# First expert's rows gathered by halves, scattered rows read back by the sync engine, one weight split moved: a two-layer diffusion block on one Trainium2 core

## The reference, cut to what matters

```python
def grouped_moe(h, router_w, router_b, w_gate, w_up, w_down):
    ...
    _, idx = lax.top_k(jnp.where(in_group, biased, NEG_INF), TOP_K)   # two experts of each token
    w = jnp.take_along_axis(scores, idx, axis=-1)
    w = w / jnp.sum(w, axis=-1, keepdims=True)
    ...
    hid = jax.nn.silu(jnp.einsum('td,edf->tef', ht, w_gate)) * jnp.einsum('td,edf->tef', ht, w_up)
    y = jnp.einsum('tef,efd->td', hid * gates[:, :, None], w_down)
```

## Time and profile before

| | |
|---|---|
| median of 3 runs | 849.35 us (847.86 to 852.73) |
| profiled execution | 854.77 us, its span 852.9 us |
| PE busy | 766.4 us (90%) |
| DVE / ACT / POOL busy | 522.3 / 470.0 / 192.3 us |
| mean granted PE clock | 0.933 |

### The profile page before, as it was taken

How to read it: one execution, slowest core, us unless ns; L and a number is a source line. 1 busy time by engine, 2 the same in 40 slices (tenths; PEclk the granted TensorE clock), 3 DMA queues, 4 the chain that set the end, 5 groups by cost and what they waited for, 6 DMA issues and landing times.

```text
span 852.9 us, 13041 instructions
## 1 busy us (share of the span) xinstructions
PE 766.4 (90%) x4850; PEld 608.9 (71%) x4850; DVE 522.3 (61%) x769; ACT 470.0 (55%) x664; POOL 192.3 (23%) x181
## 2 busy tenths in 40 slices
PE   4599999999999748999999739999999799999995
PEld 3278867856787637888888526898569588888883
DVE  2254333349733635888889436753684758988884
ACT  3353221259613625888888427641773557767763
POOL 0103000630004035699942141303102000000000
PEclk9889999999999657999999959999999689999998
DMA  9992787895111155999999879941434038999942
GB/s 361 348 262 88 268 323 270 320 310 182 51 66 50 49 199 181 322 369 361 354 364 335 307 265 304 312 149 50 170 104 159 29 142 312 366 350 345 344 164 76
DMA packets 88385, 200.06 MB, mean 235 GB/s; under 512 B 19410, under 2 KB 45564, under 8 KB 88316
## 3 DMA queue, kind: packets, MB, share of 16 engines
q1 hardware_dynamic: 81696, 185.17, 61.2%
q0 software_dynamic: 4608, 8.40, 2.8%
q10 hardware_dynamic: 2012, 5.61, 1.7%
HBM read 196.00 MB, written 11.53 MB: 243 GB/s over the span
## 4 chain that ended last, share of the span: by engine, by line
PE 66%; POOL 8%; DVE 8%; ACT 6%; DMA 6%; issue 4%; SPq 0%; ACTq 0%; POOLq 0%; DVEq 0%
PE bank L1368 13%; PE bank L1369 12%; PE bank L1370 12%; POOL onehot L875 4%; PE bank L1396 4%; DMA y_rows<-y_sb,idx_row 3%; PE bank L1525 2%; POOL x_row L885 2%; PE bank L1526 2%; PE bank L1527 2%; PE bank L1672 2%; PE bank L1698 2%; PE bank L1684 2%; DVE w_lo L2342 2%; POOL y_rows L891 1%
## 5 line engine op out<-in xcount | busy, mean ns | idle before, releaser
L2342 DVE TENSOR_TENSOR w_lo<-raw,w_hi 128x2048 fp32r<-128x2048 f32 x96 | 219.8, 2293 | 16.6 <-ACT w_hi L1234 15.8
L1234 ACT ACTIVATE w_hi<-raw 128x2048 fp32r<-128x2048 f32 x96 | 184.1, 1919 | 37.8 <-PE bank L1370 37.8
L1368 PE MATMUL bank<-h_hi,w_hi 128*128 128x512 f32 (+2 forms) x288 | 104.0, 361 | 6.4 <-DVE h_lo L2102 4.3
L1369 PE MATMUL bank<-h_lo,w_hi 128*128 128x512 f32 (+2 forms) x288 | 101.4, 352 | 0.0
L1370 PE MATMUL bank<-h_hi,w_lo 128*128 128x512 f32 (+2 forms) x288 | 101.3, 352 | 0.0
L1368 PE MATMUL bank<-w_hi,xg_hi 128*128 128x512 f32 x192 | 79.2, 413 | 2.6 <-DVE xg_lo L2506 2.6
L1369 PE MATMUL bank<-w_lo,xg_hi 128*128 128x512 f32 x192 | 76.6, 399 | 0.0
L1370 PE MATMUL bank<-w_hi,xg_lo 128*128 128x512 f32 x192 | 76.4, 398 | 0.0
L970 ACT ACTIVATE w_hi<-raw 128x2048 fp32r<-128x2048 f32 (+1 forms) x20 | 37.3, 1867 | 68.7 <-PE bank L1370 55.2
L2045 DVE TENSOR_TENSOR w_lo<-raw,w_hi 128x2048 fp32r<-128x2048 f32 (+1 forms) x20 | 44.9, 2247 | 48.4 <-ACT w_hi L970 48.2
L1368 PEld LDWEIGHTS bank<-h_hi,w_hi 128*128 128x128 f32 (+1 forms) x288 | 54.2, 188 | 16.5 <-issue 6.3
(11 more groups left out here) (326 smaller groups left out, 1547.5 us busy)
## 6 DMA issues: line engine op xcount, KB each, us to landing
raw<-in_ada_w SPq DMA_DIRECT2D x46, 1024.0 KB, 9.7
raw<-in_moe_w_gate SPq DMA_DIRECT2D x64, 512.0 KB, 5.1
raw<-in_moe_w_up SPq DMA_DIRECT2D x64, 512.0 KB
raw<-in_moe_w_down SPq DMA_DIRECT2D x64, 512.0 KB
raw<-in_w_in SPq DMA_DIRECT2D x14, 1024.0 KB, 10.9
raw<-in_w_out SPq DMA_DIRECT2D x8, 1024.0 KB, 9.3
ada_first<-in_ada_w SPq DMA_DIRECT2D x2, 1024.0 KB, 18.6
h_rows<-h_full SPq DMA_DIRECT2D x2, 1024.0 KB, 4.6
```

The lines of the kernel that those rows point to most:

```text
L1234: act.activation(w_hi[slot][:, :, :], raw[q][:, :, :], ACT.Copy).then_inc(split_hi, 1)
L1368: pe.matmul(dst, w_hi_, x_hi_, start=first, stop=False)
L1369: pe.matmul(dst, w_hi_, x_lo_, start=False, stop=False)
L2342: dve.tensor_tensor(w_lo[slot][:, :, :], raw[q][:, :, :], w_hi[slot][:, :, :].bitcast(F32), ALU.subtract).then_inc(split_lo, 1)
```

## The change

It has three parts and some renamed semaphores.

1. SP stores each column half twice: to its own tensor `h_half[half]` (T x 512), signalled by `h_first` or `h_second`, and to `h_rows` as before. POOL gathers experts 0 and 1 in four transfers of 2 KB rows: half 0 of both, then half 1 of both. PE, ACT and DVE turn and split half 0 of expert 0 first; PE multiplies role 0; then it turns half 1 of expert 0, then expert 1, and multiplies role 1. ACT's load of the SiLU table moves between the halves. Experts 2 to 15 are as before.
2. SP issues the read-back of `y_rows`, behind its six block loads. The lower half waits for all scatters but expert 15's, the upper for that one too. POOL runs `swap(1)` without a wait for the scatters. The sums are made by half tiles, 128x512: DVE makes the first, POOL the other seven.
3. DVE runs rows and modulation 1 ahead of `split(0, N_ADA)`, which moves behind the second `nx`.

```diff
@@ SP
                             sp.wait_ge(q_ta, l * KC + 4 * (half + 1))
+                            sp.dma_start(h_half[half].rearrange("(t p) d -> p t d", p=P), h_full[:, :, cs]).then_inc((h_first, h_second)[half], 16)
                             sp.dma_start(h_rows.rearrange("(t p) d -> p t d", p=P)[:, :, cs], h_full[:, :, cs]).then_inc(h_out, 16)
...
                         load_block(l + 1, q)
+                    rows = y_rows.rearrange("(i t p) d -> p t i d", i=2, p=P)
+                    sp.wait_ge(q_out[0], 16 * (E // 2) * k)
+                    sp.wait_ge(q_out[1], 16 * (E // 2) * k - 16)
+                    sp.dma_start(y_back[:, :, 0, :], rows[:, :, 0, :]).then_inc(q_lower, 16)
+                    sp.wait_ge(q_out[1], 16 * (E // 2) * k)
+                    for t in range(4):
+                        sp.dma_start(y_back[:, t, 1, :], rows[:, t, 1, :]).then_inc(q_back[t], 16)
@@ POOL
-                    gather(k, 0)
-                    gather(k, 1)
+                        gather(k, 0)
+                        gather(k, 1)
+                    else:
+                        for half in range(2):
+                            gather(0, 0, half)
+                            gather(0, 1, half)
...
-                def all_stored(n):
-                    pool.wait_ge(q_out[0], 16 * (E // 2) * n)
-                    pool.wait_ge(q_out[1], 16 * (E // 2) * n - 16)
-                    pool.sem_inc(y_in, 1)
-                    pool.wait_ge(q_out[1], 16 * (E // 2) * n)
-                    pool.sem_inc(y_in, 1)
+                def sum_rows():
                     swap(l + 1)
                     pool.wait_ge(q_lower, 16 * (l + 1))
-                    for t in range(nt):
-                        pool.wait_ge(q_back[t], 16 * (l + 1))
-                        pool.tensor_tensor(y_back[:, t, 0, :], y_back[:, t, 0, :], y_back[:, t, 1, :], ALU.add).then_inc(q_c, 1)
+                    for t, half in combine_units(l):
+                        if half == 0:
+                            pool.wait_ge(q_back[t], 16 * (l + 1))
+                        if (t, half) != (0, 0):
+                            hs = slice(half * 512, (half + 1) * 512)
+                            pool.tensor_tensor(y_back[:, t, 0, hs], y_back[:, t, 0, hs], y_back[:, t, 1, hs], ALU.add).then_inc(q_c, 1)
@@ ACT
-                    act.wait_ge(y_in, 2 * l - 1)
-                    act.dma_start(y_back[:, :, 0, :], rows[:, :, 0, :]).then_inc(q_lower, 16)
-                    act.wait_ge(y_in, 2 * l)
-                    for t in range(4):
-                        act.dma_start(y_back[:, t, 1, :], rows[:, t, 1, :]).then_inc(q_back[t], 16)
...
-                    tokens_in(0, 0)
+                        tokens_in(0, 0)
+                    else:
+                        tokens_in(0, 0, 0)
+                        act.activation(col[:, 45:46], eps, ACT.Silu)
+                        tokens_in(0, 0, 1)
@@ PE
                                 if role == 1 and e == 0:
+                                    if k == 0:
+                                        tokens(0, 0, 1)
                                     pe.wait_ge(i_row, m * (E // 2) + 2)
                                     tokens(i, j + 1)
+                                    if k == 0:
+                                        pe.wait_ge(x_hi, 1)
+                                        pe.wait_ge(x_lo, 1)
...
-                    tokens(0, 0)
+                    tokens(0, 0, None if k else 0)
@@ DVE
+                if u == 0:
+                    dve.wait_ge(q_lower, 16 * (l + 1))
+                    dve.wait_ge(q_back[0], 16 * (l + 1))
+                    dve.tensor_tensor(y_back[:, 0, 0, 0:512], y_back[:, 0, 0, 0:512], y_back[:, 0, 1, 0:512], ALU.add).then_inc(q_first, 1)
...
+                    if i == 0 and k == 1:
+                        split(0, N_ADA)
...
                     take_modulation(0, bank[START_BANK[0]])
-                    split(0, N_ADA)
                     take_rows(1, bank[START_BANK[1]])
...
-                    tokens_in(0, 0)
+                    tokens_in(0, 0, None if k else 0)
                     if k == 0:
                         further_rounds_and_rows()
+                        tokens_in(0, 0, 1)
```

More of the change, by code:

```diff
@@ L269, in build @@
         h_rows = nc.dram_tensor("h_rows", (T, D), F32, kind="Internal").ap()
+        h_half = [nc.dram_tensor(f"h_half{i}", (T, 512), F32, kind="Internal").ap() for i in range(2)]
         y_rows = nc.dram_tensor("y_rows", (2 * T, D), F32, kind="Internal").ap()
@@ L877, in one_hot, with gather @@
                     ins.then_inc(q_p, 1)
-                def gather(k, e):
-                    pool.wait_ge(h_out, 32)
+                def gather(k, e, half=None):
+                    if half is None:
+                        pool.wait_ge(h_out, 32)
+                    else:
+                        pool.wait_ge((h_first, h_second)[half], 16)
                     pool.wait_ge(i_row, k * (E // 2) + e // 2 + 1)
@@ L884, in gather @@
                         pool.wait_ge(g_lo, k * E + e - 1)
-                    pool.indirect_dma_start(x_row[e % 2][:, :], None, h_rows, bass.IndirectOffsetOnAxis(ap=idx_row[:, e, 0:1], axis=0),
-                                            bounds_check=T - 1, oob_is_err=False).then_inc(x_in[e % 2], 16)
+                    cs = slice(0, D) if half is None else slice(half * 512, (half + 1) * 512)
+                    pool.indirect_dma_start(x_row[e % 2][:, cs], None, h_rows if half is None else h_half[half], bass.IndirectOffsetOnAxis(ap=idx_row[:, e, 0:1], axis=0),
+                                            bounds_check=T - 1, oob_is_err=False).then_inc(x_first if (half, e) == (0, 0) else x_in[e % 2], 16)
                 def scatter(k, e):
@@ L1251, in rows_out, with tokens_in @@
                         act.activation(y_sb[par][:, 512:1024], bank[7][:, :], ACT.Copy).then_inc(q_ya, 1)
-                    def tokens_in(i, j):
-                        act.wait_ge(g_hi, 2 * i + (m * E + j + 1))
-                        act.wait_ge(g_lo, 2 * i + (m * E + j + 1))
+                    def tokens_in(i, j, half=None):
+                        if half != 1:
+                            act.wait_ge(g_hi, 2 * i + (m * E + j + 1))
+                        if half != 0:
+                            act.wait_ge(g_lo, 2 * i + (m * E + j + 1))
                         sl = slice(j % 2 * SLOTS, (j % 2 + 1) * SLOTS)
-                        for b in range(2):
+                        for b in range(2) if half is None else (half,):
                             ins = act.activation(xg_hi[:, 4 * b:4 * b + 4, sl],
                                                  bank[2 * (j % 2) + b][:, :].rearrange("p (c n) -> p c n", n=SLOTS), ACT.Copy)
-                        ins.then_inc(x_hi, 1)
+                        ins.then_inc(x_first_hi if half == 0 else x_hi, 1)
                     def step(i, j, e):
-                        if k == 0 and e == 0:
-                            act.activation(col[:, 45:46], eps, ACT.Silu)
                         if e is None or 2 <= e < E:
@@ L1835, in row_numbers, with tokens @@
                         ins.then_inc(i_mm, 1)
-                    def tokens(i, j):
-                        pe.wait_ge(x_in[j % 2], 16 * (i + j // 2) + 16 * (m * (E // 2) + 1))
-                        for b in range(2):
+                    def tokens(i, j, half=None):
+                        if half == 0:
+                            pe.wait_ge(x_first, 16)
+                        else:
+                            pe.wait_ge(x_in[j % 2], 16 * (i + j // 2) + 16 * (m * (E // 2) + 1 + j % 2))
+                        for b in range(2) if half is None else (half,):
                             for c in range(4):
@@ L2499, in one_round, with tokens_in @@
                     m, s0, n0 = round_start(l, k)
-                    def tokens_in(i, j):
-                        dve.wait_ge(x_hi, 2 * i + (m * E + j + 1))
+                    def tokens_in(i, j, half=None):
+                        if half == 0:
+                            dve.wait_ge(x_first_hi, 1)
+                        else:
+                            dve.wait_ge(x_hi, 2 * i + (m * E + j + 1))
                         sl = slice(j % 2 * SLOTS, (j % 2 + 1) * SLOTS)
-                        for b in range(2):
+                        for b in range(2) if half is None else (half,):
                             ins = dve.tensor_tensor(xg_lo[:, 4 * b:4 * b + 4, sl],
@@ L2508, in tokens_in @@
                                                     xg_hi[:, 4 * b:4 * b + 4, sl].bitcast(F32), ALU.subtract)
-                        ins.then_inc(x_lo, 1)
+                        ins.then_inc(x_first_lo if half == 0 else x_lo, 1)
                     def step(i, j, e):
```

43 lines of the change are left out of this document (25 added, 18 removed).

## The result

| | before | after |
|---|---|---|
| median | 851.04 us (847.86 to 855.41, 4 runs) | 843.07 us (839.02 to 845.73, 4 runs) |
| profiled execution, its span | 854.77, 852.9 us | 841.64, 839.8 us |
| ratio, with its 95% interval | | 0.990 (0.9858 to 0.9942) |

The time is outside the range of 831.5 to 842; the direction was right. The same kernel timed twice more gave 0.989 (0.9849 to 0.9931) and 0.9924 (0.99 to 0.9948), so 6.5 to 9.4 us are gained.

A forecast was written before the change was run, and what follows sets the result against it. PE is busy 90% of the span, so time can be won only in its holes, three of them touched; 0.4 + 5.4 + 8.3 = 14.1 us off the 849.35 us base gives 835.3 us, range 831.5 to 842.

The forecast's parts named there:

- 0.4 + 5.4 + 8.3: Gains in us at the start (part 3), the first gathers (part 1) and between the layers (part 2), 14.1 in all.
- 5.3, landed at 310.0: Part 1: expert 0's first half gather, issued at 304.7, takes 5.3 us and lands at 310.0.
- rival 1: First gathers: halves queue behind the doubled stores, part 1 gains only 1.0 us, total time 839.7 us; chance 0.16.
- that run begins at a row-number signal from PE, so it moves with PE: Part 1: POOL's nearly full stretch from 349 to 430 us, 19.05 of 20 us busy, shifts earlier along with PE.
- PE at full clock in expert 1 some 5 us earlier than before: A sign expected in the profile after, at expert 1: PE reaches full clock some 5 us earlier.
- rival 3: Experts 1 and 2: PE stays at 1.2 GHz, each costs 10 us more, total time 855.2 us; chance 0.04.
- 0.4, bounds 0 and 0.7: Start: with modulation ahead of the split, the first `nh` starts at 39.87 instead of 40.25 us, 0.4 gained.
- so it costs nothing: Start: the moved split's 2.3 us behind the second `nx` are covered by DVE's wait for `h_hi`, ending at 41.6.
- 8.3, bounds 4.9 and 8.8: Between the layers: PE starts the first sum's turn at 498.9 instead of 507.21 us, 8.3 gained.
- DVE, not the data, is last: Between the layers: the first upper tile arrives at 497 us, DVE is free only at about 498.1.
- into idle DMA engines: Between the layers: the 2 MB lower read, sent near 488.5 us, flows at 0.41 MB/us and is in by 495.3.
- quad 10: Between the layers: its load moves only 6 to 7 us; PE's slack of about 3 us takes the 2 us difference.

The follow-up runs named there:

- e7: The changed kernel, with DVE's first weight split of layer 0 waiting for POOL's four small copies (swap): 841.2 us, ratio 0.9908.
- e1: The changed kernel again with no edit, for an interval and a second profile: 843.62 us, ratio 0.989.
- e2: Only part 1 (half stores, half gathers, half turns), the other two parts undone: 851.36 us, ratio 0.9987.
- e13: The changed kernel once more with no edit, timed beside e12 on the same chip: 845.12 us, ratio 0.9924.
- e3: Only part 2 (read-back on SP, free swap, half sums), the other two parts undone: 847.94 us, ratio 0.9953.
- e4: Only part 3 (second modulation ahead of the weight split), the other two parts undone: 852.18 us, ratio 0.9983.
- e6: The changed kernel, with the two stores to h_rows held until the first half gather has landed: 842.12 us, ratio 0.991.
- e12: The changed kernel with the edits of e6 and e9 alone: 836.46 us, ratio 0.9833.
- e9: The changed kernel, with the one-hot tiles of pairs 2 to 7 built on DVE in place of POOL: 841.63 us, ratio 0.9895.
- e5: The changed kernel, with scatters issued earlier in POOL's order, odd experts' between the halves of its one-hot work: 845.88 us, ratio 0.9957.
- e8: The changed kernel, with the scattered rows read back by tiles, lower tiles 0 and 1 first: 843.27 us, ratio 0.9927.
- e10: The changed kernel with the edits of e6, e7 (both layers), e8 and e9 together: 834.86 us, ratio 0.9803.

## Why the prediction was wrong

- **The sum, by places.** Forecast 0.4 + 5.4 + 8.3. The stretches give: start 0.5 or 2.8, in five profiles each (the copies of e7); part 1 1.2 (first row number to expert 15, mean of after, e1, e2, e13 against before, e3, e4: 175.8 and 177.0); part 2 5.7 (last scatter to `nx`, nine profiles with it 27.7, three without 33.5). With the mean of the two starts that is 8.6; timed were 6.5 to 9.4. Part 1's 1.2 is itself a sum of three things, of which the prediction had only the first: 1.5 by expert 0, 2.4 from the clock behind it, and 2.7 given back at experts 4 and 5.
- **First failed step, part 1: "5.3, landed at 310.0".** The half gather took 8.55 us. This was my rival 1, "the halves queue behind the doubled stores", with 0.16: the earlier trace rows had it right, and the earlier trace rows, where both queues ran side by side, did not carry over. e6 shows it. At the end of expert 1's turns, where I counted 5.4 us, 1.5 were won (means of after, e1, e13 and of before, e3, e4); rival 1 had left 1.0. With the queue gone, e6 and e12 have 4.7 to 4.8 there, so the chain of steps was sound. The rest is role 0, put at 4.61 us and measured at 5.46, since the clock no longer rises within it.
- **Second failed step, part 1: "that run begins at a row-number signal from PE, so it moves with PE".** The prediction had seen POOL at 19.05 of 20 us at 360 to 380 and took it for harmless. Only the start of the run is PE's signal; its length is POOL's own, and it grew: beside the one-hot work of pair 3 DVE was busy for 12.49 of 12.99 us, before for 8.13 of 10.29. By expert 1 PE came 4.7 us earlier; POOL's scatter 1 only 2.1 (360.85 against 362.91). That POOL's load gives the gain back is shown by e9 (work taken off POOL, give-back gone) against e5 (order changed, give-back stays).
- **Luck, part 1: the clock.** "PE at full clock in expert 1 some 5 us earlier than before" came true, but nothing in the sum paid for it. The prediction weighed the clock only as a loss (rival 3); it gave 2.4 us by expert 1, twice what is left of part 1 in the end. It came in eleven of the twelve profiles with part 1, and in none of the three without.
- **Part 3, 0.4, bounds 0 and 0.7.** The cap was rightly seen in ACT's second split, wrongly as fixed: it waits for POOL's copies, and those take 2.8 or 0.76 us. The moved split was put in at "so it costs nothing", with its cover; but to move it also moved what it meets. The bound of 0.7 was no bound.
- **Third failed step, part 2, 8.3, bounds 4.9 and 8.8.** The chain is as forecast and the last element isn't: "DVE, not the data, is last" was false in every profile with part 2 but e8's (waits of 0.16 to 3.0 us). I let the lower read flow "into idle DMA engines" at 0.41 MB/us from its issue; a read's packets ran at full rate only 2.8 us after issue (486.51 to 489.3), by when the upper tiles were nearly permitted (sent from 489.65). After's DMA by queue at 491 to 497 us has 2.45 MB of q1 in 6 us: the rate was right, the start was not. And the lower permission, 1.0 us behind the last scatter's issue by my estimate, came 1.2 to 3.0 us behind it. The baseline was a chance too: before's 19.7 us from scatter to sum was 17.4 and 19.2 in e4 and e2, whose code there is the same.
- **The rest held:** the gather is issued at 303.88 (forecast 304.7, less 0.75 by which the row numbers came sooner), PE nowhere waits for quad 10, and POOL's seven sums come at 1.3 us (1.17 forecast).

## What to carry to other kernels

An engine at 95% in the windows behind a place that gets faster is the next bound, whatever starts its run: ask what it would have to do earlier, and take work off it before counting the gain. A transfer that is made ready earlier meets what is then in the queues; look at the queue at the new moment, not the old. And where two engines' instructions have two durations in one trace (0.76 and 2.8 us, 4.67 and 12.99), an order that keeps them apart can be worth more than the move itself. Last, look at the granted clock before you credit a gain to the step that you moved: here 2.4 of the 3.9 us at expert 1 were the clock's.

## What the runs showed of the hardware

- POOL's instructions on SBUF stretch beside DVE's two-operand ones: four copies 0.76 against 2.8 us, eight compares 4.67 against 12.99, an indirect transfer's issue 1.0 against 3.1. The Trainium skill, "SBUF — State Buffer" (SBUF: two separate sides), states an exclusive lock of the pair of ports that a DVE operation with two SBUF inputs and a GpSimd one share, where the loser blocks. The two timelines under e7 agree: beside the split, POOL's copies began 0.2 us ahead of it and ended 0.3 us after it.
- q0 got nothing while q1 had all of the engines: in after, at 303 to 310 us, 1008 packets of q1 (101.8% of the engines) and none of q0. The first gather, issued at 303.88, had its first packet at 310.3; in e6, issued at 303.48, at 307.1. The prediction had weighed the alternation of queues in the Trainium skill, "DMA: Bandwidth & Descriptors" (Queues, rings and completion order), for its 310.0. The measurement decides against its use here; why the engines didn't alternate, and whether the profile's packets are those that the page means, no run shows.
- The granted clock fell behind expert 0 in the four profiles in which PE stood 2.2 us there (before, e3, e4 at once, e10 in two pieces), and in none of the eleven in which it stood 1.33 to 1.41 us. Expert 0 to 1 then took 11.0 to 12.1 us instead of 9.3 to 9.5. No run changes this wait alone, so that it decides the fall isn't shown.
- About 160 us behind the first `nx` of layer 1 the clock was still 0.50 in five of 15 executions and full in ten, worth some 3 us. What decides it was not found. A single pair of profiles can't size a change of 1%.
